# First attention on raw tokens and unscaled latents, its norm's weights loaded first, and the last gate's loads placed between down units

## The reference, cut to what matters

```python
hn = rmsnorm(h, norm_attn)                      # h = x
a = hn @ w_in                                   # 1024 -> 384 + 256 + 32
c_q = rmsnorm(a[..., :384], norm_q_lat)
c_kv = rmsnorm(a[..., 384:640], norm_kv_lat)
k_pe = a[..., 640:]
q = (c_q @ w_q_up).reshape(b, s, 8, 96)
kv = (c_kv @ w_kv_up).reshape(b, s, 8, 64 + 64)
k = concat(k_nope, broadcast(k_pe))             # 64 + 32
q, k = rmsnorm(q, qk_norm_q), rmsnorm(k, qk_norm_k)   # then rotary on the last 32
w = softmax(where(mask, q k^T / sqrt(96), -inf))      # 8 heads, causal
h = h + (w v) @ w_out
```

## Time and profile before

| | us |
|---|---|
| median of the timed runs | 1131.08 (1130.45, 1131.08, 1134.28) |
| profiled execution | 1131.92 |
| its span | 1129.8 |
| PE busy | 1077.9 (95%) |
| DVE busy | 338.3 (30%) |
| ACT busy | 223.7 (20%) |
| start of the input projection | 12.08 |
| start of the first scores (behind the masks) | 59.54 |
| start of the last down group | 1088.29 |

### The profile page before, as it was taken

The page is one execution under the profiler, slowest core; times in us unless marked ns, Lnnn a source line. Parts: engine busy times, 40 slices in busy tenths (PEclk is TensorE's granted clock), DMA queues, the critical chain, the costliest instruction groups (busy, mean ns, idle before and its releaser), DMA issues.

```text
span 1129.8 us, 18872 instructions
## 1 busy us (share of the span) xinstructions
PE 1077.9 (95%) x8311; PEld 549.4 (49%) x8312; DVE 338.3 (30%) x541; ACT 223.7 (20%) x324; POOL 9.4 (1%) x53
## 2 busy tenths in 40 slices
PE   7899999999999899999999999999999999999758
PEld 5566888887688455343333343333333333333216
DVE  4654766665641525101201110100200201001043
ACT  3353444443612512000000000000000000000033
POOL 3000000000000000000000000000000000000000
PEclk9999999999999999999999999999999999999979
DMA  9806565655222309999999999999999999999951
GB/s 334 311 1 214 180 203 187 193 181 185 112 76 76 147 4 398 413 390 347 417 419 419 418 419 419 418 418 420 417 420 404 416 420 419 417 420 419 417 235 38
DMA packets 114016, 343.47 MB, mean 304 GB/s; under 512 B 7757, under 2 KB 30858, under 8 KB 113930
## 3 DMA queue, kind: packets, MB, share of 16 engines
q1 hardware_dynamic: 113930, 342.22, 77.3%
HBM read 341.15 MB, written 1.05 MB: 303 GB/s over the span
## 4 chain that ended last, share of the span: by engine, by line
PE 88%; DVE 3%; DMA 3%; SPq 3%; ACT 2%; issue 1%; DVEq 0%; ACTq 0%
PE ps L1961 33%; PE ps L1982 12%; PE ps L1686 7%; PE ps L1987 4%; PE ps L1687 4%; PE ps L1636 4%; DMA wring<-in_w_exp_down 3%; SPq L381 3%; PE ps L1666 3%; PE ps L1668 3%; PE ps L1667 3%; PE ps L1816 2%; PE ps L1938 1%; PE ps L2000 1%; PE ps L1510 1%; PE ps L1532 1%
## 5 line engine op out<-in xcount | busy, mean ns | idle before, releaser
L1961 PE MATMUL ps<-wring,xg 128*32 128x512 f32 (+1 forms) x4032 | 406.9, 559 | 4.2 <-DMA wring<-in_w_exp_gu 2.7
L1961 PEld LDWEIGHTS ps<-wring,xg 128*32 128x32 f32 x4032 | 131.0, 110 | 267.4 <-issue 258.8
L1982 PE MATMUL ps<-wring,ehT 128*32 128x512 f32 x1408 | 166.4, 601 | 14.4 <-DMA wring<-in_w_exp_down 14.4
L1686 PE MATMUL ps<-dn,w_high 128*128 128x512 f32 x352 | 124.9, 399 | 0.0
L1352 DVE TENSOR_TENSOR e_h<-e_silu,ps 128x768 f32<-128x768 f32 (+3 forms) x24 | 19.1, 796 | 345.3 <-ACT e_silu L819 345.3
L819 ACT ACTIVATE e_silu<-ps 128x768 f32<-128x768 f32 (+3 forms) x24 | 16.4, 684 | 482.7 <-PE ps L1961 482.7
L1982 PEld LDWEIGHTS ps<-wring,ehT 128*32 128x32 f32 x1408 | 44.5, 111 | 115.1 <-issue 93.2
L1102 DVE TENSOR_TENSOR w_low<-ring,w_high 128x2048 fp32r<-128x2048 f32 x36 | 82.2, 2291 | 57.0 <-ACT w_high L695 57.0
L1687 PE MATMUL ps<-dn,w_low 128*128 128x256 f32 x352 | 98.9, 281 | 0.0
L695 ACT CAST w_high<-ring 128x2048 fp32r<-128x2048 f32 x36 | 68.3, 1907 | 37.0 <-PE ps L1687 19.9
L1686 PEld LDWEIGHTS ps<-dn,w_high 128*128 128x128 f32 x352 | 66.1, 188 | 17.3 <-DVE dn L1111 0.8
(11 more groups left out here) (300 smaller groups left out, 916.7 us busy)
## 6 DMA issues: line engine op xcount, KB each, us to landing
wring<-in_w_exp_gu SPq DMA_DIRECT2D x128, 1024.0 KB, 17.7
wring<-in_w_exp_down SPq DMA_DIRECT2D x88, 1024.0 KB, 16.6
wring<-in_w_exp_gu SPq DMA_DIRECT2D x64, 768.0 KB, 14.8
ring<-in_w_ffn_gu SPq DMA_DIRECT2D x44, 512.0 KB, 4.9
ring<-in_w_ffn_down SPq DMA_DIRECT2D x11, 1024.0 KB, 5.4
ring<-in_w_ple_gate SPq DMA_DIRECT2D x4, 1024.0 KB, 4.8
ring<-in_w_q_b SPq DMA_DIRECT2D x4, 1024.0 KB, 4.8
ring<-in_w_o_b SPq DMA_DIRECT2D x4, 1024.0 KB, 5.0
```

Source lines behind the costliest of these rows:

```text
L1686: pe.matmul(bank, wh[:, kk, cols], dn[:, k].rearrange("p i t -> p (i t)"), start=(k == 0), stop=False)
L1961: ins = pe.matmul(ps[32 * j:32 * j + 32, b, 0:64 * GROUPS[g][1]], xg[:, member(n), k, 32 * b:32 * b + 32], cols, start=first, stop=last)
L1982: ins = pe.matmul(ps[32 * q:32 * q + 32, 3, :], turned(2 * u + r, b), w[:, r, half * 512:(half + 1) * 512], start=(g == 0 and u == 0 and r ...
```

## The change

- **Loads at the start.** The seven gain loads and the positions are issued by ScalarE ahead of its first table load; the first layer's attention gains have a semaphore of their own (`first_gains_in`). SyncE issues x's tile 0, two units of input weights, x's tile 1, and the rest in the old order.
- **Raw tokens.** TensorE transposes x as loaded. VectorE multiplies by the gains only. The root r of each token's mean square is computed all the same, but used later. TensorE transposes eight gains first, and all of them at k-step 6 of tile 0, with x's tile 1; the latents of tile 0 are transposed at k-step 6 of tile 1.
- **Unscaled latents.** ScalarE and VectorE copy the latents out of PSUM. Sums of squares are taken of the unscaled values and multiplied by r squared. `lat_scale` (the latents' root times r) goes into v (ScalarE's copy becomes a product), into the keys' scales, and into the queries' scale.
- **Queries.** ScalarE copies the queries out of PSUM, VectorE rotates the copies, TensorE transposes them; sums, mean and root for both tiles follow together, and the result, with 1/sqrt(96), is the scale of the exponential per query and head, and with a minus sign the factor of the row maximum.
- **Order.** Keys and values of a tile come ahead of its queries on TensorE; keys' heads ahead of queries' heads. ScalarE's and VectorE's orders follow.
- **The end.** The four gate loads go ahead of the units (down 1, 2), (down 1, 3), (down 2, 0) and (down 2, 1), one each. ScalarE's, VectorE's and TensorE's programs at the end are as before.

```diff
+        load_x(0)
+        unit_dma(sp_, *order[0], 0)
+        unit_dma(sp_, *order[1], 1)
+        load_x(1)
+        for u in range(2, 6):
...
+        at = ALONE.index(("down", 1, 2))
+        loads("end", ALONE[:at], E - 1, lambda i: e, "end")
+        for u in range(4):
+            gate_load(u, E, True)
+            loads("end", ALONE[at:at + 1], E - 1, lambda i: e, "end", at)
+            at += 1
+        loads("end", ALONE[at:], E - 1, lambda i: e, "end", at)
...
+            act.dma_start(gains_raw[r0:r0 + n, :], a[w].rearrange("l (k d) -> (l k) d", d=P)).then_inc(gains_in if i else first_gains_in, 16)
...
         load_ln_exp()
-        norm(0)
+        norm_tile(0, 0)
         act.wait_ge(angles_done, 1)
         act.activation(sincos[:].rearrange("p s t i -> p (s t i)"), red[:].rearrange("p s t i -> p (s t i)"), ACT.Sin).then_inc(trig_done, 1)
         load_ln_exp()
+        norm_tile(0, 1)
         for t in range(NT):
             act.wait_ge(a_ready, t + 1)
+            act.copy(lat[:, t, 0:QL], ps[:, 2 * t, 0:QL]).then_inc(lat_copied, 1)
             if t:
                 act.wait_ge(lat_sq_done, 3)
+            else:
+                act.wait_ge(sq_done, NT)
             act.activation(junk[:, 0:QL], ps[:, 2 * t, 0:QL], ACT.Square, accum_out=lat_sq[:, t, 0:1]).then_inc(lat_sq_done, 1)
...
+            kv = banks(4 + 2 * t, 6 + 2 * t).rearrange("p (h c) -> p h c", c=NOPE + VD)
+            act.activation(k_squares[:].rearrange("p (h c) -> p h c", c=NOPE), kv[:, :, 0:NOPE], ACT.Square).then_inc(k_squared, 1)
+            act.wait_ge(lat_scale_ready, t + 1)
+            act.mul(va[:, t], kv[:, :, NOPE:], lat_scale[:, t, 1:2])
+            if t:
+                turned_keys(0)
+            rsqrt_seed(r_qk(1, t), qk_rstd[:, 1, t, :])
+            if t:
+                turned_queries(0)
             act.wait_ge(q_done, t + 1)
             act.wait_ge(lat_sq_done, 3 * NT)
             if t:
-                act.wait_ge(squares_read, t)
+                act.wait_ge(squares_read, 2)
+            act.copy(qk[:, 0, t].rearrange("p (b h) c -> p b (h c)", b=2), ps[:, 2 * t:2 * t + 2, 0:4 * QK]).then_inc(q_copied, 1)
...
+        turned_keys(1)
+        turned_queries(1)
+        act.wait_ge(mean_ready, r_qk(0, 1) + 1)
+        both = mean_sq[:, r_qk(0, 0):r_qk(0, 1) + 1, :]
+        link(act.activation(qk_rstd[:, 0], both, ACT.Ln))
+        act.activation(qk_rstd[:, 0], qk_rstd[:, 0], ACT.Exp, scale=-0.5).then_inc(seed_ready, 2)
...
+        def latents(t):
+            dve.wait_ge(a_ready, t + 1)
+            dve.tensor_copy(kpe[:, t, :], ps[:, 2 * t + 1, KVL:KVL + ROPE])
+            dve.tensor_copy(lat[:, t, QL:], ps[:, 2 * t + 1, 0:KVL]).then_inc(lat_copied, 1)
+            dve.wait_ge(lat_copied, 2 * t + 2)
...
+        def latent_scales(t):
+            r = rstd[:, 0, t:t + 1]
+            dve.wait_ge(hs_done, t + 1)
+            link(dve.tensor_tensor(norm_sq[:, t:t + 1], r, r, ALU.mult))
+            dve.wait_ge(lat_sq_done, 3 * (t + 1))
+            for i, width in enumerate((QL, KVL)):
+                dve.tensor_scalar(lat_sq[:, t, i:i + 1], lat_sq[:, t, i:i + 1], norm_sq[:, t:t + 1], None, ALU.mult)
+            link(dve.tensor_scalar(kpe_sq[:, t:t + 1], kpe_sq[:, t:t + 1], norm_sq[:, t:t + 1], None, ALU.mult))
+            means(r_lat(t), ((lat_sq[:, t, 0:1], QL), (lat_sq[:, t, 1:2], KVL)))
+            refine(r_lat(t), lat_rstd[:, t, :])
+            link(dve.tensor_scalar(lat_scale[:, t, :], lat_rstd[:, t, :], r, None, ALU.mult))
+            dve.tensor_tensor(lat_scale_sq[:, t, :], lat_scale[:, t, :], lat_scale[:, t, :], ALU.mult).then_inc(lat_scale_ready, 1)
...
+            link(dve.tensor_scalar(qk_sq[:, 1, t, :], qk_sq[:, 1, t, :], lat_scale_sq[:, t, 1:2], kpe_sq[:, t:t + 1], ALU.mult, ALU.add))
+            means(r_qk(1, t), ((qk_sq[:, 1, t, :], QK),))
+            refine(r_qk(1, t), qk_rstd[:, 1, t, :])
+            if t:
+                dve.wait_ge(k_scaled, t)
+            dve.tensor_scalar(k_scale[:, 0, :], qk_rstd[:, 1, t, :], lat_scale[:, t, 1:2], None, ALU.mult)
+            link(dve.tensor_scalar(k_scale[:, 1, :], qk_rstd[:, 1, t, :], rstd[:, 0, t:t + 1], None, ALU.mult))
...
+        def query_scales():
+            dve.wait_ge(squares_read, 2 * NT)
+            for t in range(NT):
+                ins = dve.tensor_scalar(qk_sq[:, 0, t, :], qk_sq[:, 0, t, :], lat_scale_sq[:, t, 0:1], 1.0 / QK, ALU.mult, ALU.mult)
+            link(ins)
+            m = mean_sq[:, r_qk(0, 0):r_qk(0, 1) + 1, :]
+            dve.tensor_scalar(m, qk_sq[:, 0], EPS, None, ALU.add).then_inc(mean_ready, 2)
+            y, w = qk_rstd[:, 0], newton_q[:]
...
+            for t in range(NT):
+                ins = dve.tensor_scalar(q_scale[:, t, :], y[:, t, :], lat_scale[:, t, 0:1], 1.0 / math.sqrt(QK), ALU.mult, ALU.mult)
+            link(ins)
+            link(dve.tensor_scalar(neg_q_scale[:], q_scale[:], -1.0, None, ALU.mult))
...
+        latents(0)
+        latents_turned(0)
+        latent_scales(0)
+        latents(1)
+        latents_turned(1)
+        latent_scales(1)
+        keys(0)
+        queries(0)
+        query_squares(0)
+        keys_turned(0)
+        keys(1)
+        queries(1)
+        keys_turned(1)
+        query_squares(1)
+        query_scales()
...
-            dve.tensor_scalar(neg_max[:, j], row_max[:, j], -1.0 / math.sqrt(QK), None, ALU.mult).then_inc(sc_read, 1)
+            dve.tensor_tensor(neg_max[:, j], row_max[:, j], neg_q_scale[:, :, 2 * j:2 * j + 2], ALU.mult).then_inc(sc_read, 1)
...
+        def turn_input(t):
+            pe.wait_ge(x_in[t], 16)
+            for half in range(2):
+                for c in range(4):
+                    kk = 4 * half + c
+                    ins = pe.transpose(ps[:, norm_bank(0, t) + half, c * P:(c + 1) * P], h[:, t, kk * P:(kk + 1) * P], ident[:])
+                ins.then_inc(hT_done, 1)
...
+        pe.wait_ge(first_gains_in, 16)
+        pe.transpose(ps[:, 0, 0:8], gains_raw[0:8, :], ident[0:8, 0:8]).then_inc(gains_T, 1)
+        turn_input(0)
...
+                if k == 6:
+                    if t == 0:
+                        pe.wait_ge(gains_in, 16 * 6)
+                        pe.wait_ge(hnT_done, 2)
+                        pe.transpose(ps[:, 4, 0:NGAIN], gains_raw[:, :], ident[0:NGAIN, 0:NGAIN]).then_inc(gains_T, 1)
+                        turn_input(1)
+                    else:
+                        turn_latents(0)
...
+                if half == 1:
+                    ins.then_inc(q_done, 1)
+                elif t:
+                    turn_heads(0, 0)
...
+        keys_values(0)
+        turn_latents(1)
         queries(0)
-        turn_latents(1)
+        keys_values(1)
+        turn_heads(1, 0)
         queries(1)
-        keys_values(0)
-        turn_heads(0, 0)
-        keys_values(1)
+        turn_heads(1, 1)
         turn_heads(0, 1)
```

216 lines of the change are left out of this document (110 added, 106 removed).

## The result

The changed kernel takes 1127.79 us (median of 7 runs, 1124.12 to 1130.09) against 1131.56 for the kernel before (7 runs, 1130.45 to 1134.28): ratio 0.9968, interval 0.9953 to 0.9984. It is faster, by 3.8 us instead of 7.0. The profiled execution took 1127.49, its span 1125.4.

What follows compares the result with a forecast made beforehand. Expert stage bound by its weights at 418 GB/s, earlier stages by the engines. Front 7.0 us and tail 0 off the profiled 1131.92 gave 1124.9, off the timed median 1124.1; predicted 1124.3 us, range 1119.8 to 1128.8.

Steps and rivals of the forecast that it cites:

- the first scores: First attention on TensorE, after the masks: start at 51.7 us instead of 59.54, with 0.8 us taken off for hand-overs.
- the front's 7.0: Start through first scores: 7.0 us saved, bounds 3.5 and 8.5, moving all later stages equally.
- The tail's 0: Last expert's down group with gate loads set between its units: 0 us gained, bounds -1.3 and +1.85.
- The rule weighed there: Last down group: work shorter than the wait for weights leaves the array cold; by it the tail loses 1.3 us.
- these 1.7 us are in the 7.8 saved: Head turn and masks before the first scores: the lower clock's 1.7 us counted within the 7.8 us saved.
- cost nothing, bounds -0.3 and +0.3: Attention exponentials scaled by a column instead of a constant: 0 us, bounds -0.3 and +0.3 for 16 exponents.
- A: Rival: clock falls again ahead of the masks and VectorE's chain is longer; saving 3.8 us, 1127.3; chance 0.17.
- B: Rival: front at its full 7.8 us plus tail at the higher clock 1.85; saving 9.6, 1121.5; chance 0.12.
- C: Rival: late rotary gains or first weights hold the input projection; saving under 3 us, 1129; chance 0.08.
- D: Rival: last down group's units all at 1.2 GHz, tail loses 1.3 us; saving 5.7, 1125.4; chance 0.16.
- E: Rival: TensorE stays at 1.2 GHz through the input projection, 15.6 us more; slower, 1139.7; chance 0.05.
- the shift at 100 us differing from the shift at 1060 us by over 1 us: Sign of being wrong, early attention against late experts: would mean the expert stream doesn't follow the front.

Runs made afterwards that it cites:

- kernel before again: The kernel before run once more, unchanged, against the kernel before: 1131.88 us, ratio 1.0002.
- three pauses filled: Kernel before with dummy identity transposes on TensorE before the second norm's transposes, before the first gate product and after the third norm's transposes: 1129.06 us, 0.9991.
- experiment 4: Kernel before with only the last gate's loads moved: 1129.97 us, 0.9991; changed kernel with those loads back in the old order: 1128.19 us, 0.9972.
- Experiment 8: Changed kernel with TensorE waiting for all seven gain loads before its first transpose, as in the kernel before: 1131.78 us, 0.9996.
- experiment 3: Changed kernel with attention exponentials scaled by an immediate number instead of a column: 1124.66 us, 0.9942 to the kernel before.
- all five fillings: Changed kernel with dummy transposes in three pauses between dense projection and shared expert, ahead of the input projection and in the last down group: 1121.36 us, 0.9914.
- The shifts of 3 and 6 us: Changed kernel with 27 or 54 dummy transposes ahead of the first attention output product: 1128.73 us, 0.9980, and 1130.14 us, 0.9996.
- the masks' pause filled: Kernel before with 14 dummy transposes in TensorE's pause ahead of the last turn of heads, before the first masks: 1131.02 us, 0.9996.

## Why the prediction was wrong

**The right steps.** The first input matmul (forecast 7.1, measured 7.29; that is 4.6 us sooner than the timeline's 11.87, where the forecast counted from the chain's 12.08), the clock back near 11, the projection's end (29.0; 29.39), no wait on a weight load, the rotary tables well before the latents, three waits of TensorE on VectorE between 40 and 51, all under 1 us, the first scores (51.7 and 0.8 for hand-overs; 52.35). As working on the one profiled execution the front's 7.0 was good: 7.2 at the first scores. (Its lower bound of 3.5 adds up to 3.0 from its own three parts.) The tail's 0 measured 0 to 1, inside its bounds. In the tail the units set apart took 1.92 to 3.37 us, and the pair behind the last wait 5.23 where the batch of three took 7.67. The rule weighed there, of the Trainium skill's "TensorE: Matmul & The Clock Gate", section "HAM oscillation — how this bites in real kernels" (runs of tiles rather than single ones between waits), would by the forecast's reading of it have had the units apart all low. The trace agrees for one of the four rows above (3.37) and in part for two (2.60, 5.23); the unit behind a wait of 1.56 us took 1.93.

**The step that failed** is the front's term of 7.0 as a saving of the *kernel*, with its sentence that every later stage shifts by the same amount. It read the earlier trace rows as the kernel's own, and 2.8 us of them belonged to that execution: this is the number that the forecast had wrong, and it lies in the kernel before. From the two profiles of the kernel before: the input pair at 12 us took 1.49 us in one and 0.81 in the other, and the way from it to the queries' first product 21.2 against 20.0 us (to 33.11 and 31.79); the masks' group took 2.12 against 1.46, behind a low head turn. The forecast said of the latter that "these 1.7 us are in the 7.8 saved". They were not there to be saved in every execution, and an execution without them paid 1.5 us at the gates' group and 1.6 at the shared product instead, which the earlier trace rows can't show: they leave out the time from 280 to 540.

Four profiles have the front as in the kernel before (durations in us; the low part of the dense product is given by its start):

```
                              input pair   masks   low part   gates' group   shared product
kernel before (forecast's)       1.49      2.12     282.40       3.70            3.84
the tail's edit alone            1.49      1.97     281.99       3.70            5.47
kernel before again              0.81      1.46     279.58       5.21            5.47
three pauses filled              0.81      1.46     279.43       filled          filled
```

Two of four have the front's falls, and the forecast's is the only unfilled one without any fall behind it. The six profiles with the changed start and nothing else edited ahead of it reach the low part at 275.29 to 276.33. Against the two fronts without falls that is 3.1 to 4.3 us.

Set against the execution that falls where the changed kernel's falls, the shift is even up to the experts:

```
                              before again    changed    shift
first input matmul                11.79         7.29      4.50
attention output product          74.64        71.16      3.48
dense product's low part         279.58       276.00      3.58
gates' first group               288.51       284.93      3.58
shared product                   328.94       325.41      3.53
first expert's first unit        438.45       435.15      3.30
last expert's first down unit   1069.44      1064.08      5.36
last gate product               1104.08      1098.75      5.33
```

So the front is worth 3.5 us between executions that fall in the same places, and the tail nothing here, 0 to 1 by experiment 4: with the measured 3.8 the account closes within the noise. (The spans of these two executions are 5.4 apart, because their expert stages differ by 2.1; see the last section.) How often each kernel has which falls isn't known from so few profiles, so the median's 3.8 is not worked out from shares. Of the front the start alone brings 4.5. Experiment 8 has 3.45 for the gains' wait in the changed kernel, of which 0.9 is the last gain's later landing (7.92 for 7.02). From the first input matmul to the last head turn the changed kernel takes 0.3 us longer than this execution: the low clock and the transposes inside the projection give back what unscaled latents and copied queries save. And 0.7 to 0.9 goes to the exponentials, forecast "cost nothing, bounds -0.3 and +0.3": a second and smaller miss, a term mis-sized (experiment 3).

**The rivals.** A gave 1127.3, nearly the time, which is luck, for it has the wrong place: no profile of a form of the changed kernel (12 of them) has low masks. It had the right kind of cause, a fall behind a pause, but put it into the front. B's 9.6 us are nearly what the change with all five fillings brings (9.7), by another sum. C, D and E did not come. (E's 17.8 us for 16 low steps should be 18.1 by its own 1.13 a step; nothing rests on it.) Of the signs that I named, "the shift at 100 us differing from the shift at 1060 us by over 1 us" came true (6.3 at the attention output product, 3.3 at the last expert) and its reading was wrong: the expert stream did follow the front, from the first expert to the last.

**Open.** What decides whether a pause ends at 1.2 GHz. Of the ten profiles with high masks and the gates' pauses unfilled seven have the gates' group low. Of the two with low masks neither has, but one of them has the shared product low. That product is low in ten of the twelve profiles in which its pause is unfilled, the forecast's being one of the two others. The shifts of 3 and 6 us fit neither a fixed time nor this order alone, and one to three profiles of each form can't settle shares.

## What to carry to other kernels

One profile is one execution: before a stretch of it is booked as a saving, look in a second profile whether its slow matmuls are there again, and take the difference from two executions that fall in the same places. This holds for a result too: the tail's 1.1 us in the first pair of profiles are not there in the second. After a saving upstream, read every TensorE pause behind it, not only the stage that sets the pace; with equal waits and longer matmuls the loss is the clock's, and some idle-time transposes test it in one run and may well be kept. Fill only real pauses: in a batch without one, and ahead of further waits, the same transposes went with a slower kernel before.

## What the runs showed of the hardware

- TensorE's pauses of 1.20 and 0.94 us, one soon after the other, and of 2.14 us were followed by 1.2 GHz in some executions of one program (the kernel before) and by 2.4 in others, each fall costing 1.5 to 1.7 us (5.21 to 5.40 for 3.70, 5.47 for 3.84).
- The 31 runs of the kernel before in one comparison go from 1128.6 to 1135.3 us. With the masks' pause filled, 12 runs lie in two groups: four from 1127.8 to 1128.4 (mean clock 0.994), eight from 1130.8 to 1133.1 (0.987 to 0.991). A median then depends on the share of the groups as much as on a cost.
- A ScalarE exponential on 128x128 whose scale is a column takes 0.47 us, with a number 0.38; on 128x256 0.57 and 0.49.
- The seven gain loads, issued by ScalarE from 0.78 us on beside the first weights, were all there at 7.92 us; issued by SyncE from 1.71 us on ahead of the weights, at 7.0.
- Between profiled executions the expert stage, from its first unit to the last expert's first down unit, took 627.3 to 631.4 us, a spread as large as the change's worth; no experiment went after that.
- The way from there to the last gate product took 34.6 to 35.8 us with the last three down units in one batch behind a wait of 10.5 us, and 34.1 to 36.1 with them apart.
